# A hybrid GLA/SSD and sparse-attention trunk: the opening is rebuilt, and the bias line and parameters move to phase two of the first FFN

## What is computed

```python
def rmsnorm(x, g):
    y = xf * lax.rsqrt(jnp.mean(xf * xf, axis=-1, keepdims=True) + EPS)
    return (y * g.astype(jnp.float32)).astype(x.dtype)

def swiglu(h, wg, wu, wd):
    return (jax.nn.silu(h @ wg) * (h @ wu)) @ wd
# per layer: x += 1/2 swiglu(rmsnorm(x)); x += mixer(rmsnorm(x)); x += 1/2 swiglu(rmsnorm(x))
```

## Time and profile before

| | us |
|---|---|
| median of 3 runs (2265.01 to 2270.43) | 2266.13 |
| the profiled execution | 2266.44 |
| its span | 2264.6 |
| PE busy | 2171.9 (96%) |
| first unit begins on PE | 28.59 |
| third unit begins on PE | 43.97 |
| busy DVE, ACT | 1243.0, 724.2 |
| PE idle in the slices of the page that show a 6 | in the first and in the fourth 56.6 us |

### The profile page before, as it was taken

How to read it: one execution, slowest core, us unless ns; L and a number is a source line. 1 busy time by engine, 2 the same in 40 slices (tenths; PEclk the granted TensorE clock), 3 DMA queues, 4 the chain that set the end, 5 groups by cost and what they waited for, 6 DMA issues and landing times.

```text
span 2264.6 us, 28156 instructions
## 1 busy us (share of the span) xinstructions
PE 2171.9 (96%) x10212; PEld 1780.3 (79%) x10212; DVE 1243.0 (55%) x2008; ACT 724.2 (32%) x998; POOL 49.4 (2%) x87
## 2 busy tenths in 40 slices
PE   6996999999999999999999999999997999999998
PEld 5885788788878777888888888888765778888886
DVE  6532535588556898534446544535668535535445
ACT  3221222432423544212224222223355653222222
POOL 0000000000000000000000000000001210000000
PEclk8998999999999999999999999999998999999999
DMA  4339333331124325433333333332310003333321
GB/s 142 93 103 135 104 95 83 103 84 46 50 73 125 85 71 161 118 97 94 97 95 100 93 99 96 94 101 83 94 40 20 1 29 93 93 102 94 101 81 68
DMA packets 362749, 200.23 MB, mean 88 GB/s; under 512 B 13507, under 2 KB 356678, under 8 KB 362662
## 3 DMA queue, kind: packets, MB, share of 16 engines
q1 hardware_dynamic: 359238, 184.73, 28.4%
q0 software_dynamic: 3424, 14.35, 3.7%
HBM read 191.55 MB, written 7.37 MB: 88 GB/s over the span
## 4 chain that ended last, share of the span: by engine, by line
PE 85%; DVE 9%; DMA 3%; issue 1%; ACT 1%; SPq 1%; DVEq 0%; ACTq 0%
PE ps L1387 24%; PE ps L1388 24%; PE ps L1389 24%; DMA w_raw<-in_ffn_w_gate 2%; PE ps L1769 2%; PE ps L1791 1%; PE ps L1509 1%; DVE w_lo L740 1%; PE ps L1406 1%; PE ps L1407 1%; PE ps L1408 1%; DVE index_scores L1277 1%; PE ps L1760 1%; DVE stat L1260 1%; DVE index_scores L1262 1%
## 5 line engine op out<-in xcount | busy, mean ns | idle before, releaser
L445 ACT ACTIVATE w_hi<-w_raw 128x1024 fp32r<-128x1024 f32 x351 | 371.7, 1060 | 1121.2 <-PE ps L1389 1033.6
L1387 PE MATMUL ps<-h_hi,w_hi 128*128 128x512 f32 x1704 | 668.7, 392 | 23.2 <-DVE silu_gate L859 20.9
L1388 PE MATMUL ps<-h_lo,w_hi 128*128 128x512 f32 x1704 | 665.5, 391 | 0.0
L1389 PE MATMUL ps<-h_hi,w_lo 128*128 128x512 f32 x1704 | 665.2, 390 | 0.0
L740 DVE TENSOR_TENSOR w_lo<-w_raw,w_hi 128x1024 fp32r<-128x1024 f32 x351 | 428.8, 1222 | 321.2 <-ACT w_hi L445 321.1
L1387 PEld LDWEIGHTS ps<-h_hi,w_hi 128*128 128x128 f32 x1704 | 321.5, 189 | 91.6 <-DVE w_lo L740 23.4
L1389 PEld LDWEIGHTS ps<-h_hi,w_lo 128*128 128x128 f32 x1704 | 321.4, 189 | 67.3
L1388 PEld LDWEIGHTS ps<-h_lo,w_hi 128*128 128x128 f32 x1704 | 321.4, 189 | 66.2
L1387 PE MATMUL ps<-act_hi,w_hi 128*128 128x512 f32 x704 | 273.9, 389 | 0.0
L1388 PE MATMUL ps<-act_lo,w_hi 128*128 128x512 f32 x704 | 273.9, 389 | 0.0
L1389 PE MATMUL ps<-act_hi,w_lo 128*128 128x512 f32 x704 | 273.9, 389 | 0.0
(11 more groups left out here) (273 smaller groups left out, 2045.0 us busy)
## 6 DMA issues: line engine op xcount, KB each, us to landing
w_raw<-in_ffn_w_gate SPq DMA_DIRECT2D x88, 512.0 KB, 3.8
w_raw<-in_ffn_w_up SPq DMA_DIRECT2D x88, 512.0 KB, 3.8
w_raw<-in_ffn_w_down SPq DMA_DIRECT2D x64, 512.0 KB, 3.9
w_raw<-in_hy_w_in SPq DMA_DIRECT2D x44, 512.0 KB, 3.8
w_raw<-in_ffn_w_down SPq DMA_DIRECT2D x32, 384.0 KB, 3.4
w_raw<-in_hy_w_out SPq DMA_DIRECT2D x16, 512.0 KB, 4.0
line_scratch<-line POOLq DMA_DIRECT2D x1, 5120.0 KB, 55.1
acum_rows<-acum_scratch POOLq DMA_DIRECT2D x4, 1024.0 KB, 10.5
```

The source lines that it names most:

```text
L445: act.activation(w_hi[:, s, :], w_raw[:, s, :], ACT.Copy).then_inc(hi_ready, 1)
L1387: pe.matmul(ps[:, bank, :], wh, rh[:, k, :], start=k == 0, stop=False)
L1388: pe.matmul(ps[:, bank, :], wh, rl[:, k, :], start=False, stop=False)
L1389: mm = pe.matmul(ps[:, bank, :], wl, rh[:, k, :], start=False, stop=k == nk - 1)
```

## The change

In the opening:

- SP issues the 32 rows of FFN gains first, then x in two halves of 512 channels with the first gate tile between them, then the first up tile, and only behind the third and fourth weight tiles the other eight parameter rows and the eight of other shapes.
- PE turns the FFN gains by themselves, and the first half of x as soon as it has landed, in six banks (2 to 7). The first two units are interleaved with the transposes and run in step, block by block (`very_first_units`).
- ACT makes `h_hi` straight from the PSUM bank, DVE makes `h_lo` from the same bank, and DVE's copy to `x` (`keep_x`) comes later and releases the bank. The copies of tiles 0 and 1 release banks 2 and 3 for the transposes of tiles 6 and 7.
- The squares come from the token-major `x_in`: four activations of 128x1024 with an accumulated sum for each token; `rsqrt` reads them from `rs`. The eight squares, seven additions and PE's sums over partitions of this norm are gone.

In phase two of the same FFN: the bias line and the turning of the parameters are done between the gate/up units and the down units (`bias_line_and_params`, `line_out`), in banks 6 and 7. So POOL's wait for `l_ev` now ends there. The third down unit of that phase waits until ACT has emptied these banks.

```diff
-                sp.dma_start(x_in[:, :, :], a["x"][0].rearrange("(t p) d -> p t d", p=P)).then_inc(x_landed, 16)
+                sp.dma_start(prow[0:32, 0, :], a["ffn_norm_g"]...).then_inc(ffn_gain_landed, 16)
+                sp.dma_start(x_in[:, :, 0:D // 2], x_rows[:, :, 0:D // 2]).then_inc(x_landed[0], 16)
+                sp.dma_start(slot(0), first_gate).then_inc(raw_landed[0], 16)
+                sp.dma_start(x_in[:, :, D // 2:D], x_rows[:, :, D // 2:D]).then_inc(x_landed[1], 16)
+                sp.dma_start(slot(1), first_up).then_inc(raw_landed[1], 16)
...
-                            for j in range(4):
+                            for j in range(2, 4):
                                 load(j, 0, [(slot(j), (g_src, u_src)[j % 2][:, :, (j // 2) * P:(j // 2 + 1) * P])])
+                                row_params()
                                 column_params()
...
+            def squares(t):
+                act.wait_ge(x_landed[0], 16)
+                act.wait_ge(x_landed[1], 16)
+                return act.activation(squared_x[:, t, :], x_in[:, t, :], ACT.Square, accum_out=rs[:, 3, t:t + 1])
+            def line_out():
+                act.wait_ge(l_mm, 1)
+                act.activation(line[:, 0:TOK], ps[0:AH, 6, :], ACT.Copy).then_inc(l_ev, 1)
+                act.wait_ge(par_done, 2)
+                act.activation(line[:, TOK:LINE], ps[0:AH, 7, 0:P], ACT.Copy).then_inc(l_ev, 1)
+                act.activation(gains[:, 32:83], ps[:, 7, P + 32:P + 83], ACT.Copy).then_inc(gains_ready, 1)
+                act.activation(gains[:, GB_CW:GB_CW + 48], ps[:, 7, 2 * P:2 * P + 48], ACT.Copy).then_inc(gains_ready, 1)
...
             for m in range(KT):
-                next_x(STAGES[0], 0, m)
-                if m in (2, 4, 6):
-                    produce_hi(m // 2)
+                act.wait_ge(xt_done, m + 1)
+                act.activation(h_hi[:, m, :], ps[:, 2 + m % 6, :], ACT.Copy, scale=gains[:, m:m + 1]).then_inc(ohi_done, 1)
+                if m < 2:
+                    produce_hi(m)
+                if m in (3, 4, 5):
+                    squares(m - 3)
+                if m == 6:
+                    produce_hi(2)
+            squares(3).then_inc(ss_done, 1)
+            produce_hi(3)
...
             for m in range(KT):
-                dve.wait_ge(xt_done, m + 1)
-                dve.tensor_copy(x[:, m, :], ps[:, 4 + m % 4, :]).then_inc(x_upd, 1)
-            produce_lo(0)
...
+                first_low(m)
+                if m < 2:
+                    produce_lo(m)
+                if m in (2, 3):
+                    keep_x(m - 2)
+            for m in range(2, KT):
+                keep_x(m)
+                if m == 4:
+                    produce_lo(2)
+            rsqrt(0, TT, 1.0 / D)
+            produce_lo(3)
...
+                for m in range(4):
+                    turn(m)
+                block(0, 0)
+                turn(4)
+                turn(5)
+                block(0, 1)
+                block(0, 2)
+                turn(6)
+                turn(7)
+                block(1, 0)
+                block(1, 1)
+                block(1, 2)
+                for k in range(3, KT - 1):
+                    block(0, k)
+                    block(1, k)
+                block(0, KT - 1)
+                block(1, KT - 1)
+                pe.wait_ge(x_upd, KT)
+                spread(NORMS[STAGES[0]], [SPREAD_BANK(STAGES[0])])
...
+            def bias_line_and_params():
+                pe.wait_ge(l_landed, 32)
+                pe.wait_ge(x_upd, 2 * KT)
+                pe.matmul(ps[0:AH, 6, :], rel_bias_sb[:, :], bucket_sb[:, 0:TOK], start=True, stop=True)
+                pe.matmul(ps[0:AH, 7, 0:P], rel_bias_sb[:, :], bucket_sb[:, TOK:LINE], start=True, stop=True, skip_group_check=True).then_inc(l_mm, 1)
+                pe.wait_ge(par_landed, 16 * 8)
+                pe.transpose(ps[:, 7, P:P + 83], prow[0:83, 0, :], ident[0:83, 0:83]).then_inc(par_done, 1)
+                pe.transpose(ps[:, 7, 2 * P:2 * P + 48], prow[0:48, 1, :], ident[0:48, 0:48]).then_inc(par_done, 1)
```

More of the change, by code:

```diff
@@ L485, in ffn @@
                     n += 2 * nf
+                    if st == STAGES[0] and ph == 1:
+                        line_out()
                     if ph < 2:
@@ L1319, in mix1 @@
                 last_updates(XB["mix1"], n + NU["mix1"] - KT, 1.0, nxt)
+            dve.sem_inc(sq_ready, KT)
+            dve.sem_inc(sq_added, KT - 1)
             dve.sem_inc(mul_done, 1)
@@ L1341, in _, with first_low, keep_x @@
             mstep(dve.tensor_scalar(masks[:, LEVELS, :], ij[:, 2, :], 0.0, None, ALU.is_equal))
[L1342 to L1357 removed]
+            def first_low(m):
+                dve.wait_ge(ohi_done, m + 1)
+                dve.scalar_tensor_tensor(out=h_lo[:, m, :], in0=ps[:, 2 + m % 6, :], scalar=gains[:, m:m + 1],
+                                         in1=h_hi[:, m, :].bitcast(F32), op0=ALU.mult, op1=ALU.subtract).then_inc(opnd_ready, 1)
+            def keep_x(m):
+                dve.tensor_copy(x[:, m, :], ps[:, 2 + m % 6, :]).then_inc(x_upd, 1)
+            dve.wait_ge(gains_ready, 1)
+            for m in range(KT):
+                first_low(m)
[9 more added lines that the diff above has]
+            produce_lo(3)
             for k, st in enumerate(STAGES):
@@ L1416, in first_units, with very_first_units, turn, block @@
                 spread(NORMS[st], [SPREAD_BANK(st)])
+            def very_first_units():
+                def turn(m):
+                    pe.wait_ge(x_landed[m // 4], 16)
+                    if m >= 6:
+                        pe.wait_ge(x_upd, m - 5)
+                    for t in range(TT):
+                        mm = pe.transpose(ps[:, 2 + m % 6, t * P:(t + 1) * P], x_in[:, t, m * P:(m + 1) * P], ident[:, :])
+                    mm.then_inc(xt_done, 1)
+                def block(u, k):
+                    if k == 0:
+                        pe.wait_ge(gains_ready, 1)
+                        pe.wait_ge(lo_ready, u + 1)
+                    if u == 0:
+                        pe.wait_ge(opnd_ready, k + 1)
+                    wh, wl = w_hi[:, u, k * P:(k + 1) * P], w_lo[:, u, k * P:(k + 1) * P]
+                    pe.matmul(ps[:, u, :], wh, h_hi[:, k, :], start=k == 0, stop=False)
+                    pe.matmul(ps[:, u, :], wh, h_lo[:, k, :], start=False, stop=False)
+                    mm = pe.matmul(ps[:, u, :], wl, h_hi[:, k, :], start=False, stop=k == KT - 1)
+                    if k == KT - 1:
+                        mm.then_inc(unit_used, 1)
+                for m in range(4):
[17 more added lines that the diff above has]
+                spread(NORMS[STAGES[0]], [SPREAD_BANK(STAGES[0])])
@@ L1467, in ffn @@
                     n += 2 * nf
+                    if st == STAGES[0] and ph == 1:
+                        bias_line_and_params()
                     pe.wait_ge(alo_done, f + nf - 2 + 1)
```

62 lines of the change are left out of this document (26 added, 36 removed).

## The result

The change takes 2253.11 us (median of 4 runs, 2250.52 to 2253.25), the kernel before 2265.73 beside it (4 runs, 2265.01 to 2270.43). The ratio is 0.9938, 95% interval 0.9923 to 0.9953: faster by 0.6%, which was given 0.91. The prediction of 2250 is 3.1 us low, inside its range of 2243 to 2258. The gain between the medians is 12.6 us, where the sum had 15.9. The profiled execution of the change took 2250.52 us, the shortest of its four; the last experiment bears on the other 2.6 us.

What follows compares the result with a forecast made beforehand. PE was taken as the bound from the third unit on, with two gaps to shrink. Opening -12.0, bias line +1.6 and line transfer -5.5 gave -15.9: 2266.4 to 2250.5, rounded 2250 us; range 2243 to 2258.

Steps and rivals of the forecast that it cites:

- The two gaps: PE's stands in the kernel before: the opening, and the line transfer in phase two, with 25.5 us lost.
- The opening, -12.0: Start of the kernel: third unit begins at 31.8 instead of 43.97 us; -12.0 taken, bounds -14 to -8.5.
- ACT's chain: Opening: ACT's work from weight tile two's landing at 13.3 to the last `h_hi` at 22.9, 9.6 us.
- the signs that were named: Trace signs of being right, including third unit at 31 to 33 us and ACT's longest opening wait for weight tile two.
- The bias line, +1.6: Phase two: the bias line's matmuls and two transposes add 1.6 us on PE, where nothing covers them.
- Hidden work: Opening: small parameters and the fifth weight tile, queued later, still arrive in time for unit five at 42.7 us.
- The line transfer, -5.5: Phase two, among the down units: 20.0 us lost instead of 25.5; bounds 16 to 28 lost.
- with less I expect d7 at T + 45 to 50: Phase two: the eighth down unit's weight tile lands 45 to 50 us after the last up unit's end (T).
- if d7 waits for the end too, 23: Phase two: 23 us lost if the eighth down unit's weight tile also waits until the line transfer ends.
- 16.3 + 2.7: Phase two: 16.3 us lost until PE resumes after the line transfer, plus 2.7 by the clock.
- The rule of the Trainium skill: Rival, phase two: weights get ten packets for one, so the line transfer is free; -36, 2230.5 us, chance 0.02.
- one more spell of low clock: Opening: while PE waits for `rsqrt`; one of the causes behind the bound of only -8.5 us.

Runs made afterwards that it cites:

- e10_change_again: The last experiment: the change itself, unedited, run once more beside the kernel before; 2253.10 us, ratio 0.9949.
- e12_from_x: The change with `h_hi` and `h_lo` of the opening made from `x` after DVE's copy, as in the kernel before; 2249.82 us, ratio 0.9925.
- e3_split16: The change with the line transfer cut into 16 pieces, each released by PE's unit count; 2231.93 us, ratio 0.9843.
- e8_split_order: The change with the line transfer in 16 paced pieces, `rsqrt` ahead of five copies, and ACT's and DVE's opening work reordered; 2232.42 us, ratio 0.9835.

## Why the prediction was right, and where it was not

- *What bounds.* Right. The two gaps were the ones to work on, and the third unit's date moved what stood behind it.
- *The opening, -12.0: mechanism right, size off by 1.85.* Weight tile two landed at 12.75 (13.3 taken), 0.55 of it. The step that was mis-sized most is ACT's chain, 1.0 of it: 9.6 us were taken from tile two to the last `h_hi`, and 8.6 passed (12.75 to 21.32), because consecutive instructions overlap: an `h_hi` of 0.69 us takes 0.57 in a row of ACT's work. A square with its sum is 1.05 and a read of 0.20, 1.04 together in a row; 1.06 was taken. The blocks ended at 27.2 (28.2) and `rsqrt`, at 29.09 (30.9), bound as said. Two of the signs that were named did not come: the third unit was at 30.12 and not at 31 to 33, and ACT's longest wait in the opening was not the one for weight tile two (2.79 us) but for the fifth tile (8.27), and after that for the first transposes (4.59).
- *What the gain of the opening is made of.* Half of it was read rightly: `bucket_sb` alone is 7.8 us. The prediction reckoned the edit as one chain and did not say what each part gives; `e12_from_x` shows the operands from PSUM to be worth nothing; with the late copies that go with them, they cost 0.6 us.
- *The bias line, +1.6.* Measured 1.6.
- *Hidden work.* Right for the change, with less to spare than written: "if their 9.2 us to landing were doubled it would still be in time". The fifth tile landed 11 us after its issue and ACT needed it, with `rms_rows` and the table load behind it, so that a third unit 2.2 us earlier already met it. What stands behind the waiting instruction on ACT was not counted.
- *The line transfer, -5.5: it gave -3.3.* The step that failed is "with less I expect d7 at T + 45 to 50": it landed at T + 56.9. The 34.9 us of the earlier trace rows belonged to a tile that had 563 of its packets before the line transfer was in full flow; d7 had none for its first 14 us, then one for one, and so could not end before the line transfer did. PE resumed at 296.39, T + 59.2 (T + 61.4 taken), since only one tile had to be split; one wait and not two. The line written for this case, "if d7 waits for the end too, 23", was 0.8 too high. The sum itself has a step without a reason: 16.3 + 2.7 are 19.0, and 20.0 was taken. With 19.0 the miss would be 3.2 and not 2.2.
- *The rule of the Trainium skill* on about 9 to 17 descriptors from one ring before the next ("DMA: Bandwidth & Descriptors", section "Queues, rings and completion order") was taken to give 2230.5. The trace doesn't bear out ten weight packets for one large one: 591 were served for 594, after 14 us of none at all. That is what the prediction read from its own rows, "one 512-byte packet or so for each large one", and so 0.02 was enough. The reading of the rule was at fault too, since it speaks of every ring alike; ten for ten would leave the line transfer as dear as one for one. `e3_split16` reaches that time by another way.
- *The total.* The two errors, -1.85 and +2.2, cancel, so that the profiled execution met the sum by luck. The median is 2.6 us above that execution; the bounds held "one more spell of low clock" and the predicted time did not.

## What to carry over

The large transfer on the second queue was a matter of how much of it stood there at once, not of its bytes: cut it so that one piece is shorter than the stock of tiles ahead (here 16 pieces of 4.9 us against three landed tiles of 5.44), pace it by the consumer's progress, and ask where to put it only then. When an opening is shortened, look at what each engine will wait for next and what stands behind that wait on its row; `e8_split_order` won 4.7 us on the third unit and gave back 3.6 of them 15 us later, and a spell of low clock behind it, for a tile that was issued behind parameters nobody needed yet. And a part of a rebuilding that looks like the point of it (operands from PSUM, x in halves) may be worth nothing; undoing it alone costs one run.

## What the runs showed of the hardware that was not expected

- While a software queue's 5 KB packets and 512-byte weight packets were both served, it was 591 small to 594 large and 585 to 596: by packets, not by bytes. The weights moved at 10 GB/s (0.30 MB in 30 us), where 512 KB every 5.44 us are 96.
- A weight tile issued 2.0 to 5.0 us behind the 5 MB transfer got no packet at all for some 14.5 us, in four kernels. One issued 0.8 us behind it had 563 of its packets at once. The cause is open.
- Two executions of one kernel differed by 4.7 us, and the dates place it at three half-clock spells, the first of them right behind a wait of PE. The same wait of 2.0 us was followed by such a spell in `e10_change_again` and in `e3_split16`, and by none in the first execution of the change.
- An activation with an accumulated sum is followed by a read of its own of 0.20 us; since the two overlap with their neighbours, the pair costs 1.04 us in a row.
